# A one-core MoE layer whose residual columns are stored in the order of the expert weights' rows

## What is computed

```
x = LayerNorm(alpha * x + mix(x)) with ln1_g, ln1_b           # 512 x 1024
g = argmax group of x @ w_group                               # 4 groups
two best experts of the group by x @ w_exp_router             # 8 of 32 experts each
for each expert e, over the tokens that chose it:
    h = silu(x @ w_e_gate[e]) * (x @ w_e_up[e])               # gate, up: 1024 x 512
    y = h @ w_e_down[e]                                       # down: 512 x 1024
out = LayerNorm(alpha * x + weighted sum of y) with ln2_g, ln2_b
```

## Time and profile before

| | |
|---|---|
| median of 3 runs | 1305.18 us (1303.05 to 1305.51) |
| the profiled execution | 1305.17 us, its span 1303.5 us, mean granted clock 0.986 |
| PE busy | 1262.4 us (97%) |
| DVE, ACT, POOL busy | 655.4, 406.6, 63.7 us |
| moved by DMA | 286.11 MB, 222 GB/s of HBM traffic over the span |
| chain that ended last | PE 95%, DVE 2%, ACT 1%, DMA 1% |

### The profile page before, as it was taken

How to read it: one execution, slowest core, us unless ns; L and a number is a source line. 1 busy time by engine, 2 the same in 40 slices (tenths; PEclk the granted TensorE clock), 3 DMA queues, 4 the chain that set the end, 5 groups by cost and what they waited for, 6 DMA issues and landing times.

```text
span 1303.5 us, 16037 instructions
## 1 busy us (share of the span) xinstructions
PE 1262.4 (97%) x6122; PEld 859.0 (66%) x6122; DVE 655.4 (50%) x938; ACT 406.6 (31%) x568; POOL 63.7 (5%) x70
## 2 busy tenths in 40 slices
PE   7999999999999999999999998999999999999992
PEld 6888887887888888888888887344444444444441
DVE  5496666336446347347434855144444444444447
ACT  4766755222433333333343402111111111111111
POOL 1000000000000000000015101000000000000000
PEclk9999999999999999999999997999999999999997
DMA  7322222353323323223222499899999999999991
GB/s 244 89 85 78 85 79 73 92 168 92 98 65 101 93 64 97 82 79 97 81 81 84 132 419 384 315 414 408 414 413 412 409 414 414 414 408 413 406 408 75
DMA packets 166056, 286.11 MB, mean 219 GB/s; under 512 B 9952, under 2 KB 107344, under 8 KB 166000
## 3 DMA queue, kind: packets, MB, share of 16 engines
q1 hardware_dynamic: 162224, 276.81, 57.7%
q0 software_dynamic: 2624, 4.33, 0.9%
q10 hardware_dynamic: 1152, 4.19, 0.8%
HBM read 285.17 MB, written 4.33 MB: 222 GB/s over the span
## 4 chain that ended last, share of the span: by engine, by line
PE 95%; DVE 2%; ACT 1%; DMA 1%; issue 0%; SPq 0%; DVEq 0%; ACTq 0%; POOLq 0%
PE bank L1331 19%; PE bank L1333 19%; PE bank L1332 19%; PE bank L1583 18%; PE bank L1612 9%; PE bank L1636 5%; PE bank L1573 2%; PE bank L1605 1%; PE bank L1503 1%; PE bank L1431 1%; DMA vec_rows<-in_b_merge_dram 0%; DVE x L1122 0%; DVE stats L1109 0%; DVE x L1118 0%; DMA xg<-x_dram,first_x 0%
## 5 line engine op out<-in xcount | busy, mean ns | idle before, releaser
L807 DVE TENSOR_TENSOR w_lo<-raw,w_hi 128x1024 fp32r<-128x1024 f32 x120 | 148.4, 1238 | 184.8 <-ACT w_hi L529 183.5
L1583 PE MATMUL bank<-m_raw,xe 128*64 128x512 f32 x1024 | 235.1, 602 | 0.7 <-ACT xe L529 0.7
L803 DVE TENSOR_TENSOR x<-x,bank 128x1024 f32<-128x1024 f32 x124 | 145.8, 1217 | 163.1 <-PE bank L1636 163.1
L1331 PE MATMUL bank<-xt_hi,w_hi 128*128 128x512 f32 x576 | 225.0, 391 | 2.2 <-ACT merge L618 1.0
L1333 PE MATMUL bank<-xt_hi,w_lo 128*128 128x512 f32 x576 | 224.2, 389 | 0.0
L1332 PE MATMUL bank<-xt_lo,w_hi 128*128 128x512 f32 x576 | 224.1, 389 | 0.0
L529 ACT ACTIVATE w_hi<-raw 128x1024 fp32r<-128x1024 f32 x120 | 126.2, 1057 | 172.2 <-PE bank L1333 172.1
L1583 PEld LDWEIGHTS bank<-m_raw,xe 128*64 128x64 f32 x1024 | 68.3, 137 | 129.3 <-issue 128.2
L1331 PEld LDWEIGHTS bank<-xt_hi,w_hi 128*128 128x128 f32 x576 | 108.1, 188 | 25.4 <-ACT merge L618 1.4
L1333 PEld LDWEIGHTS bank<-xt_hi,w_lo 128*128 128x128 f32 x576 | 108.1, 188 | 22.7
L1332 PEld LDWEIGHTS bank<-xt_lo,w_hi 128*128 128x128 f32 x576 | 108.2, 188 | 21.9
(11 more groups left out here) (250 smaller groups left out, 1701.6 us busy)
## 6 DMA issues: line engine op xcount, KB each, us to landing
m_raw<-in_w_e_gate_dram SPq DMA_DIRECT2D x64, 1024.0 KB, 18.7
m_raw<-in_w_e_up_dram SPq DMA_DIRECT2D x64, 1024.0 KB, 18.6
m_raw<-in_w_e_down_dram SPq DMA_DIRECT2D x64, 1024.0 KB, 18.7
raw<-in_w_in_dram SPq DMA_DIRECT2D x88, 512.0 KB, 3.9
raw<-in_w_ret_o_dram SPq DMA_DIRECT2D x16, 512.0 KB, 3.3
raw<-in_w_lru_o_dram SPq DMA_DIRECT2D x16, 384.0 KB, 3.3
raw<-in_w_out_dram SPq DMA_DIRECT2D x8, 512.0 KB, 3.7
x_rows<-in_x_dram ACTq DMA_DIRECT2D x4, 512.0 KB, 5.9
```

Source lines behind the costliest of these rows:

```text
L803: return dve.tensor_tensor(dst, a, b, op)
L807: return dve.tensor_tensor(dst, a, b_r.bitcast(F32), ALU.subtract)
L1331: pe.matmul(dst, sh, mh, start=first and x == 0, stop=False)
L1583: last = pe.matmul(bank[side:side + ROWS, 0, :], xe[:, 4 * half + k, :], w[:, FE * k:FE * k + FE], start=half == 0 and k == 0, stop=half = ...
```

## The change

`x2` is kept with permuted columns. In each half of 512 columns the stored column 128*b + p is column 4*p + b of the reference. The weights of gate and up are then read in pieces of four neighbouring rows (8 KB) and those of down in pieces of two (8 KB), one piece for a partition and unit in place of two of 4 KB.

- `turn_x` takes 128 neighbouring columns of `xg` for each transpose.
- `layer_norm` writes its first pass to PSUM (`mid`, two banks) and does its second pass in two halves of 512 columns. The first norm reads PSUM with a step of four elements and writes `x2` in the stored order; the second reads PSUM with a step of 128 and writes the reference's order.
- `y_high`, `y_low` read PSUM with a step of four elements, `gu_evict` with a step of two.
- `w_rt` is loaded in the same row order, by four DMAs in place of two. Copies of ln1_b and of ln2_g in the stored order are written to DRAM by four DMAs of 512 elements of 4 bytes each. SP waits for them before it loads ln1_b.

```
+NEAR = 4
+def by_rows(ap):
+    return ap.rearrange("q (p b) -> q b p", b=NEAR)
+def stored_rows(ap):
+    return ap.rearrange("q (b p) -> q b p", b=NEAR)
...
-        w_gate = io["w_e_gate"][0].rearrange("e (a p b) n -> p e a (b n)", p=P, b=2)
-        w_up = io["w_e_up"][0].rearrange("e (a p b) n -> p e a (b n)", p=P, b=2)
-        w_down = io["w_e_down"][0].rearrange("e (k p) n -> p e k n", p=P)
+        w_gate = io["w_e_gate"][0].rearrange("e (a p b) n -> p e a (b n)", p=P, b=NEAR)
+        w_up = io["w_e_up"][0].rearrange("e (a p b) n -> p e a (b n)", p=P, b=NEAR)
+        w_down = io["w_e_down"][0].rearrange("e (h p b) n -> p e h (b n)", p=P, b=2)
...
-            sp.dma_start(w_rt_v[:, :, 0:GROUPS], io["w_group"][0].rearrange("(k p) n -> p k n", p=P)).then_inc(router_in, 16)
-            sp.dma_start(w_rt_v[:, :, GROUPS:36], io["w_exp_router"][0].rearrange("(k p) n -> p k n", p=P)).then_inc(router_in, 16)
+            for a in range(KD // NEAR):
+                ks, rows_a = slice(NEAR * a, NEAR * a + NEAR), slice(P * NEAR * a, P * NEAR * (a + 1))
+                sp.dma_start(w_rt_v[:, ks, 0:GROUPS], io["w_group"][0][rows_a].rearrange("(p b) n -> p b n", b=NEAR)).then_inc(router_in, 16)
+                sp.dma_start(w_rt_v[:, ks, GROUPS:36], io["w_exp_router"][0][rows_a].rearrange("(p b) n -> p b n", b=NEAR)).then_inc(router_in, 16)
...
+            for dst, src in ((ln1_b_rows, io["ln1_b"]), (ln2_g_rows, io["ln2_g"])):
+                for a in range(KD // NEAR):
+                    cols = slice(P * NEAR * a, P * NEAR * (a + 1))
+                    sp.dma_start(dst[0, cols].rearrange("(b p) -> b p", p=P), src[0, cols].rearrange("(p b) -> b p", p=P),
+                                 allow_slow_non_contiguous=True).then_inc(ln_ordered, 16)
...
-            sp.dma_start(ln1[:, 1, :], row(io["ln1_b"])).then_inc(ln1_in, 16)
+            sp.wait_ge(ln_ordered, 64)
+            sp.dma_start(ln1[:, 1, :], row(ln1_b_rows)).then_inc(ln1_in, 16)
...
-                sp.dma_start(m_raw[n % MRING][:, :].rearrange("p (k n) -> p k n", k=2), src).then_inc(m_loaded[n % MRING], 16)
+                sp.dma_start(m_raw[n % MRING][:, :].rearrange("p (k n) -> p k n", k=src.shape[1]), src).then_inc(m_loaded[n % MRING], 16)
...
-                copy(gu_sb[:, :], bank[:, 0, :]).then_inc(gu_out, 1)
+                copy(gu_sb[:, :].rearrange("q (h b p) -> q h b p", b=2, p=P),
+                     bank[:, 0, :].rearrange("q (h p b) -> q h b p", b=2, p=P)).then_inc(gu_out, 1)
...
-                act.activation(dst[:, :], bank[:, b, :], ACT.Identity, scale=w).then_inc(yhi_ok, 1)
+                act.activation(stored_rows(dst[:, :]), by_rows(bank[:, b, :]), ACT.Identity, scale=w).then_inc(yhi_ok, 1)
...
-                step(dve.scalar_tensor_tensor(xt, xt, mv[:, 0:1], ln[:, 0, :], ALU.subtract, ALU.mult))
+                z, g = (v.rearrange("q (c n) -> q c n", c=2) for v in (x2[:, t, :], ln[:, 0, :]))
+                step(dve.scalar_tensor_tensor(mid, z, mv[:, 0:1], g, ALU.subtract, ALU.mult))
...
-                dve.scalar_tensor_tensor(xt, xt, scale_v[:, 1:2], ln[:, 1, :], ALU.mult, ALU.add).then_inc(ok, 1)
+                for c_ in range(2):
+                    cols = slice(512 * c_, 512 * c_ + 512)
+                    last = dve.scalar_tensor_tensor(end(x2[:, t, cols]), start(mid[:, c_, :]), scale_v[:, 1:2], end(ln[:, 1, cols]), ALU.mult, ALU.add)
+                last.then_inc(ok, 1)
...
-                rows = xg[0:ROWS, :].rearrange("r (a p b) -> r a b p", p=P, b=2)
                 for k in range(KD):
-                    last = pe.transpose(bank_x[:, k, :], rows[:, k // 2, k % 2, :], ident[0:ROWS, 0:ROWS])
+                    last = pe.transpose(bank_x[:, k, :], xg[0:ROWS, P * k:P * k + P], ident[0:ROWS, 0:ROWS])
```

More of the change, by code:

```diff
@@ L242, in layer @@
         x2_dram = nc.dram_tensor("x2_dram", [TOKENS, D], F32).ap()
+        ln1_b_rows = nc.dram_tensor("ln1_b_rows", [1, D], F32).ap()
+        ln2_g_rows = nc.dram_tensor("ln2_g_rows", [1, D], F32).ap()
         list_dram = nc.dram_tensor("list_dram", [ROWS * LIST_COLS, 1], I32).ap()
@@ L262, in layer @@
         gret_ok, acc_ok, merged, mrg_hi_ok, mrg_split = sem("gret_ok"), sem("acc_ok"), sem("merged"), sem("mrg_hi_ok"), sem("mrg_split")
-        ln1_in, res_in = sem("ln1_in"), sem("res_in")
+        ln1_in, res_in, ln_ordered = sem("ln1_in"), sem("res_in"), sem("ln_ordered")
         proj_ok, z_ok, x2_var, x2_std, x2_ok = (sem(n) for n in ("proj_ok", "z_ok", "x2_var", "x2_std", "x2_ok"))
@@ L413, in load_gate_up @@
                 for half in range(2):
-                    load_m(gu_unit(e) + 2 * half, expert(w_gate, e, 2 * half, 2 * half + 2))
-                    load_m(gu_unit(e) + 2 * half + 1, expert(w_up, e, 2 * half, 2 * half + 2))
+                    load_m(gu_unit(e) + 2 * half, expert(w_gate, e, half, half + 1))
+                    load_m(gu_unit(e) + 2 * half + 1, expert(w_up, e, half, half + 1))
             def load_down(e):
                 for half in range(2):
-                    load_m(down_unit(e) + half, expert(w_down, e, 2 * half, 2 * half + 2))
+                    load_m(down_unit(e) + half, expert(w_down, e, half, half + 1))
             load_gate_up(0)
@@ L426, in _ @@
             sp.wait_ge(m_done, M_END - MRING + 4)
-            sp.dma_start(ln2[:, 0, :], row(io["ln2_g"])).then_inc(ln2_in, 16)
+            sp.dma_start(ln2[:, 0, :], row(ln2_g_rows)).then_inc(ln2_in, 16)
             sp.dma_start(ln2[:, 1, :], row(io["ln2_b"])).then_inc(ln2_in, 16)
@@ L442, in _ @@
                             for x, w in enumerate((w_gate, w_up)):
-                                sp.dma_start(m_raw[2 * half + x][:, :].rearrange("p (k n) -> p k n", k=2),
-                                             expert(w, e, 2 * half, 2 * half + 2)).then_inc(ovf_in, 16)
+                                sp.dma_start(m_raw[2 * half + x][:, :].rearrange("p (k n) -> p k n", k=1),
+                                             expert(w, e, half, half + 1)).then_inc(ovf_in, 16)
                         for half in range(2):
-                            sp.dma_start(m_raw[4 + half][:, :].rearrange("p (k n) -> p k n", k=2),
-                                         expert(w_down, e, 2 * half, 2 * half + 2)).then_inc(ovf_in, 16)
+                            sp.dma_start(m_raw[4 + half][:, :].rearrange("p (k n) -> p k n", k=1),
+                                         expert(w_down, e, half, half + 1)).then_inc(ovf_in, 16)
             for t in range(TT):
@@ L1109, in half_stats, with layer_norm @@
                 step(dve.bn_stats(stats[:, 12 * t + 6 * half:12 * t + 6 * half + 6], x2[:, t, 512 * half:512 * half + 512]))
-            def layer_norm(t, ln, var, std, ok):
-                xt = x2[:, t, :]
+            def layer_norm(t, ln, mid, start, end, var, std, ok):
                 step.wait()
@@ L1132, in _ @@
                     if half:
-                        layer_norm(t, ln1, x2_var, x2_std, x2_ok)
-            dve.wait_ge(router_in, 64)
+                        mid = bank[:, t - 1:t + 1, :] if t else bank[:, 6:8, :]
+                        layer_norm(t, ln1, mid, by_rows, stored_rows, x2_var, x2_std, x2_ok)
+            dve.wait_ge(router_in, 96)
             dve.wait_ge(consts_ok, 1)
@@ L1273, in y_low @@
                 dve.wait_ge(yhi_ok, s + 1)
-                dve.scalar_tensor_tensor(dst[:, :], bank[:, b, :], w, high[:, :].bitcast(F32), ALU.mult, ALU.subtract).then_inc(ylo_ok, 1)
+                dve.scalar_tensor_tensor(stored_rows(dst[:, :]), by_rows(bank[:, b, :]), w, stored_rows(high[:, :].bitcast(F32)),
+                                         ALU.mult, ALU.subtract).then_inc(ylo_ok, 1)
             def add_z(a, first=False):
@@ L1321, in _ @@
                 half_stats(t, 1)
-                layer_norm(t, ln2, f_var, f_std, f_ok)
+                mid = bank[:, 0:2, :] if t % 2 == 0 else bank[:, 4:6, :]
+                layer_norm(t, ln2, mid, lambda v: v.rearrange("q (b p) -> q p b", b=NEAR),
+                           lambda v: v.rearrange("q (p b) -> q p b", b=NEAR), f_var, f_std, f_ok)
         @block.tensor
@@ L1500, in router @@
                 pe.wait_ge(x2t_ok, t + 1)
-                pe.wait_ge(router_in, 64)
+                pe.wait_ge(router_in, 96)
                 for k in range(KD):
```

## The result

The changed kernel takes 1320.36 us (median of 4 runs, 1319.93 to 1322.04), the kernel before 1305.31 on the same chip. The ratio is 1.0121, 95% interval 1.0108 to 1.0134: 15 us slower, where 1293.3 was forecast. The profiled execution took 1320.01 us, with a span of 1318.1 against 1303.5.

The account below looks back on a forecast made before the run. PE was taken as the bound, with DMA only 2.3 us of cover behind. Terms -12.9 (transposes), +0.9 and +0.1 (norms) sum to -11.9, from 1305.2 to 1293.3 us; range from 1290.5 less half a us to 1304.

Parts of the forecast that it names:

- "Cost nothing" for SP's extra issues: Ahead of the heads' first unit: six more DMAs, 3 us of issues and 1.2 us of pieces, hidden at no cost.
- The cover: At the heads' first unit: a delay up to 4 us unseen by ACT, one of 12 us hardly seen by PE.
- a gap of PE near 297 us: Sign of being wrong: PE idle where it needs the split of the heads' first unit, about 296.8 us.
- The price of 8 KB pieces: Expert weight loads: 313 ns against 324 for two of 4 KB, so a unit takes about 2.54 us, not 2.62.
- the prediction's own formula: End of expert stage: last unit lands at 825.9 plus 170 unit times, 1257.7; PE, 12.9 us ahead, asks at 1260.5.
- the rival in which 8 KB are carried as two of 4 KB: Expert weight loads: last unit still lands at 1271.1, PE's gain is capped at 2.3 us, total 1303.9; 9%.
- The transposes: Expert stage, xg: neighbouring columns cut a group of eight from 0.99 to 0.59 us, 12.9 us off over 32 groups.
- The rival that the stride was not the cause: Transposes of xg: their 64 rows make the load long, so nothing is gained, total 1306.2; 9%.
- Strided reads of PSUM: gu_evict, y_high, y_low and the norms' second pass read PSUM with a step: no cost taken.
- Last norm: Second pass as two instructions, 1.50 against 1.28 us, 0.22 more a tile: +0.9 us for four tiles.
- The largest PE gain, 1290.5: Low end of the range: xg transposes gain 0.46 us a group, 14.7 us, before half a us for spread.
- The case of slow PSUM reads: Rival: strided PSUM reads take twice as long, in the last expert and both norms, +10.1, total 1302.4; 7%.

Follow-up runs that it names:

- experiment 4: The kernel before with four DRAM-to-DRAM copies of the same bytes in natural order, 2 KB in one stretch, ahead of the heads' first loads: 1304.54 us, 0.9999.
- experiment 3: The kernel before with only two, then one, of the four scattered copies added ahead of the heads' first loads: 1312.51 us (1.0054) and 1304.48 us (0.9998).
- experiment 1: The changed kernel without the four copies; ln1_b and ln2_g loaded in natural order, with strided SBUF reads by DVE in the norms: 1302.53 us, 0.9988.
- experiment 8: The kernel of experiment 1 with each unit of expert weights in two pieces of 4 KB in place of one of 8: 1305.24 us, 1.0012.
- experiment 9: The kernel before with 8 KB weight pieces, x2 in the reference's order, no copies, transposes taking every fourth column of xg: 1304.09 us, 0.9998.
- Experiment 7: The changed kernel with GpSimd issuing one copy per head, and half the bytes of most down units from the 27th unit on left out: 1289.81 us, 0.9894.
- experiment 2: The kernel before with only the four scattered copies added ahead of the heads' first loads: 1323.12 us, 1.0148.
- experiment 5: The changed kernel with the four copies issued by GpSimd near the start of the program in place of by SP: 1312.44 us, 1.0081.

## Why the prediction was wrong, and where it was right

**"Cost nothing" for SP's extra issues: this step failed.** It had three parts. The issues: 3 us, and experiment 4 agrees. The pieces: 128 of 4 bytes for an engine at 9 ns, 1.2 us for all. The 9 ns came from a line through pieces of 512 bytes and of 4 KB, from DRAM to SBUF; it was drawn on to 4 bytes and to another kind of transfer, with no bounds, and no row was near. If a copy's elements are spread evenly over 16 engines, each has 32 of them, and the copy lands in some 11 us: 0.34 us an element, or 0.27 without the 2.3 us that a copy in one stretch takes, 30 to 38 times the price (an estimate from these landings; the spread is not shown). The cover: "one of 12 us hardly by PE" was read from the later split at 296.85; experiment 3 shows 10 us from the landing on, 5 from the start of the split. The delay, 311.33 less 284.55, was 26.8 us, PE waited 20.8 us where it had waited 0.9, some 2 us more went to the low clock behind the wait, and the stage began 20.4 us late. One copy would have been free; four in a row cost the whole loss. None of the rivals named this, though "a gap of PE near 297 us" stood among the signs of being wrong, and it is there that the gap came.

**The price of 8 KB pieces: a term of the wrong size.** Forecast were 2.54 us a unit in place of 2.62; experiment 1 gave 2.604 against the 2.622 of experiment 8, and experiment 9, with 8 KB from 824.0 to 1266.3 us, 2.60 too. The DMA share of 1.03, above all that there is, could already say that packets overlap in the records, so that their durations sum to more than a unit takes; after shows 1.01 at the same 414 GB/s. From 900 to 1200 us a record of 8 KB lasts 318 ns in the changed kernel (98.1% of 16 engines for 121.12 MB) and two of 4 KB last 325 in the one before (99.8% for 120.88 MB). So the line through two sizes, 313, was itself too low, and by these records a unit would save 0.05 us; it saved 0.02. By the prediction's own formula 2.604 puts the last landing at 825.9 + 442.7 = 1268.6, 8.1 us behind PE's 1260.5. The 12.9 shrink to 4.8, which is what was measured against the stage at full clock (6.3 against the profiled one of before). This is close to the rival in which 8 KB are carried as two of 4 KB: the capped case is what came, on top of the copies.

**What was right.** The transposes: 138 ns and 0.58 us for a group where 0.59 stood. That the 0.58 is so near is in part luck. In the group at 1020.37 us the last transpose starts at 1020.80, so the spacing is 0.061 and not 0.055, and the gap behind it 0.15 and not 0.21: two errors that cancel. The 86 ns that the prediction took as the fixed part of a weight load came from loads of which those of 128 columns last 188 ns, while the load that it was taken off lasts 140. PE's gain: 0.41 a group, 13.1 us for 32. Experiment 7, where no load holds PE up, has a stage of 443.8 us, 13.0 less than the 456.8 of experiment 9, whose PE work is the old one. The 14.5 less than before's hold the 1.5 us of clock. The rival that the stride was not the cause fell, and with it the rule of the Trainium skill (Advanced Engine Details and Errata, SBUF Cachelines) that a step is free while two accesses share a 16-byte line: for weight loads of float32 these runs show the same price at steps of two and of four, so the measurement decides against it here. For DVE experiment 1 has the penalty of a step of four. Strided reads of PSUM are free: the page of after has `y_lo` at 750 ns and `y_hi` at 688, as the rows without a step, and the first pass with its output in PSUM takes 1.28 us. Last norm: +0.5 measured, +0.9 forecast, since the two halves overlap a little (1.41 us for two of 0.75). The 0.1 of the first norm is below what the start of the stage varies by.

**Slips in its sums.** "The largest PE gain, 1290.5" leaves out the 1.0 us of the norms: 1305.2 - 14.7 + 1.0 is 1291.5, and half a us below it 1291.0. The case of slow PSUM reads adds up to 9.9 us and not 10.1, so to 1302.2. Neither changes anything in the outcome.

**What stays open.** Why one scattered copy delays the load behind it by 9.5 us and the next ones by 5 to 6 each; why the delay of the changed kernel was 5 us longer than that of experiment 2 with the same four copies; and whether reads or writes of the single elements are slow, as both were single in every run here.

## What to carry to other kernels

Price a reordering DMA by its elements and not by its bytes, and look for who else needs the DMA engines in that time: one scattered copy behind a cover of 10 us was free, four in a row cost 19 to 20 us on SP's queue, and 15 (1312.4 against 1297.8) on GpSimd's. When a faster engine eats from buffers that are filled ahead, work out the pace of both sides to a hundredth of a microsecond a unit, since the full buffers hide the difference until late in the stage. When the records of DMA already sum to more than all engines, expect a larger piece to save less than its packets say, as here. Before a difference of 1 or 2 us in a stage is put down to a change, compare the granted clock at its start in both traces.

## What the runs showed of the hardware that was not expected

- A copy of 512 separate floats from DRAM to DRAM, alone, takes 11 to 12 us to land, in one stretch of 2 KB 2.3 us. While several of them are under way, loads behind them on the same queue hardly move (1 GB/s from 280 to 300 us), though the packets' records fill only part of the engines' time, and loads of another queue land in 19.5 us in place of 4.9 (experiment 5).
- A transposing weight load of float32 with 64 rows takes 138 ns from neighbouring columns, 211 with a step of two and 213 with a step of four.
- DVE takes 1.09 to 1.12 us for 512 elements with a step of four floats in SBUF, 0.75 without; with a step in PSUM alone the time does not change.
- A wait of PE of 20.8 us costs more than its length: its granted clock was 0.50 when the work came back, and the first 4 us of products went at about half their pace.
